# A fused mixer, expert gather and second block: the mixer written for halves of the tokens, the expert loads in groups of four

## The reference, cut to what matters

```python
h = _rmsnorm(x, norm_mix_w)
proj = h @ w_in                       # q, k, v, z, two gates, pool input
qkv = silu(_causal_conv(qkv, conv_w))
o = _chunk_gated_delta_rule(q, k, v, g, beta)
pool_out = _multiscale_pool(p, w_pool, pool_scale)
x = x + concatenate([o, pool_out]) @ w_out
# experts, for each token: 8 heads, 16 experts each, from 128 x 128
q = (xb @ w_query).reshape(t, 8, 2, 128)
scores = einsum("thpc,hpkc->thpk", q, sub_keys)
s1, i1 = top_k(scores[:, :, 0], 16); s2, i2 = top_k(scores[:, :, 1], 16)
top_s, idx = ...                      # the best 16 of the 256 sums s1 + s2
gate = softmax(top_s)
act = gelu(einsum("td,thkd->thk", xb, expert_down[idx]))
x = x + einsum("thk,thkd->td", gate * act, expert_up[idx])
x = _rmsnorm(x, norm_final_w)
```

## Time and profile before

| | before |
|---|---|
| time, median of 3 runs | 2648.42 us (2647.81 to 2650.79) |
| profiled execution, its own time | 2648.01 us |
| its span | 2646.2 us |
| PE, DVE, ACT, POOL busy | 80%, 51%, 31%, 43% of the span |
| DMA | 647.63 MB, mean 245 GB/s |
| granted PE clock, mean | 0.955 |

### The profile page before, as it was taken

How to read it: one execution, slowest core, us unless ns; L and a number is a source line. 1 busy time by engine, 2 the same in 40 slices (tenths; PEclk the granted TensorE clock), 3 DMA queues, 4 the chain that set the end, 5 groups by cost and what they waited for, 6 DMA issues and landing times.

```text
span 2646.2 us, 20923 instructions
## 1 busy us (share of the span) xinstructions
PE 2120.1 (80%) x7148; PEld 1243.0 (47%) x7148; DVE 1349.2 (51%) x2765; ACT 810.2 (31%) x1865; POOL 1143.9 (43%) x826
## 2 busy tenths in 40 slices
PE   7878988957777777777777777777698886999996
PEld 4335945832222222223222232222486655788785
DVE  2446443166676776776776767765401441333301
ACT  2121212223333333333333333332423552222212
POOL 6971681344444444444444444443342002344442
PEclk8987998979999999999999999999798998999998
DMA  5441032159999999999999999997221001122221
GB/s 203 143 151 72 29 120 76 55 220 421 421 421 421 421 421 421 421 421 421 422 421 421 421 421 419 422 416 328 96 96 64 1 0 64 64 96 96 96 96 48
DMA packets 90443, 647.63 MB, mean 245 GB/s; under 512 B 10208, under 2 KB 10208, under 8 KB 19808
## 3 DMA queue, kind: packets, MB, share of 16 engines
q0 software_dynamic: 73728, 536.90, 48.8%
q1 hardware_dynamic: 16608, 109.39, 11.4%
HBM read 644.16 MB, written 2.10 MB: 244 GB/s over the span
## 4 chain that ended last, share of the span: by engine, by line
PE 48%; DMA 37%; DVE 7%; ACT 5%; POOL 2%; issue 1%; ACTq 0%; DVEq 0%; SPq 0%; POOLq 0%; PEldq 0%
PE ps L426 47%; DMA arena<-in_experts,arena_u 36%; DVE arena L1331 2%; ACT arena L873 1%; ACT sel L867 1%; ACT upper L961 1%; PE ps L385 1%; ACT arena L375 1%; DVE arena L1246 0%; DVE arena L1390 0%; DVE x L1391 0%; POOL gtrow L1009 0%; ACT sel L864 0%; DMA arena<-in_w_early 0%; DMA x<-in_x 0%
## 5 line engine op out<-in xcount | busy, mean ns | idle before, releaser
L426 PE MATMUL ps<-arena 128*128 128x512 f32 (+1 forms) x3536 | 1325.2, 524 | 406.7 <-ACT arena L873 347.7
L426 PEld LDWEIGHTS ps<-arena 128*128 128x128 f32 x3536 | 590.7, 194 | 1120.2 <-ACT arena L873 552.8
L1080 POOL DMA_INDIRECT arena<-in_experts,arena_u x512 | 601.6, 1175 | 693.5 <-PE ps L426 582.8
L1331 DVE CUSTOM_DVE_ANT_0 arena<-arena 128x1024 f32<-128x1024 f32 x512 | 627.4, 1225 | 374.2 <-DMA arena<-in_experts,arena_u 370.7
L426 PE MATMUL ps<-r_low 128*128 128x512 f32 x2208 | 511.3, 393 | 9.2 <-DVE r_low L1352 7.6
L1089 POOL TENSOR_TENSOR r_low<-middle,r_low 128x1024 fp32r<-128x1024 f32 x98 | 235.6, 2404 | 544.5 <-ACT r_low L905 544.5
L426 PEld LDWEIGHTS ps<-r_low 128*128 128x128 f32 x2208 | 415.6, 189 | 98.6 <-issue 6.5
L864 ACT ACTIVATE sel<-sel 128x2 f32<-128x2 f32 x256 | 52.1, 203 | 805.2 <-DVE sel L1331 805.2
L905 ACT ACTIVATE r_low<-middle 128x1024 fp32r<-128x1024 f32 x98 | 103.6, 1058 | 280.4 <-PE ps L426 280.3
L873 ACT ACTIVATE arena<-consts,sel 128x128 f32<-128x128 f32 x512 | 177.5, 394 | 23.5
L867 ACT ACTIVATE sel<-sel,arena 128x1 f32<-128x1 f32 x512 | 122.7, 286 | 8.4
(11 more groups left out here) (183 smaller groups left out, 1492.7 us busy)
## 6 DMA issues: line engine op xcount, KB each, us to landing
middle<-in_w_late SPq DMA_DIRECT2D x24, 2048.0 KB, 7.7
gtrow<-in_w_ada SPq DMA_DIRECT2D x32, 512.0 KB, 3.8
arena<-in_w_early SPq DMA_DIRECT2D x7, 2048.0 KB, 11.6
arena<-in_w_ada SPq DMA_DIRECT2D x32, 256.0 KB, 2.8
middle<-in_w_early SPq DMA_DIRECT2D x4, 2048.0 KB, 7.8
arena<-in_experts,arena_u POOLq DMA_INDIRECT x512, 23.9
x<-in_x SPq DMA_DIRECT2D x1, 2048.0 KB, 8.1
arena<-in_rows SPq DMA_DIRECT2D x1, 2048.0 KB, 7.1
```

The lines of the kernel that those rows point to most:

```text
L426: return nc.tensor.matmul(out_, lhsT, rhs, start=start, stop=stop_, skip_group_check=skip)
L1080: nc.gpsimd.indirect_dma_start(ring[n % RING], None, a["experts"], bass.IndirectOffsetOnAxis(ap=idxq[:, i, k:k + 1], axis=0),).then_inc(ga ...
L1331: ins = nc.vector.tensor_tensor_reduce(r[:, 0:D], r[:, 0:D], xn[:, i // PH, :], 1.0, 0.0, ALU.mult, ALU.add, dots[:, g:g + 1])
```

## The change

The mixer and the query are written for half of the tokens (`SH` = 256 columns, two chunks), as a list of small stages (`STAGES`, made by `front_plan`), which every engine walks in the same order. The first half's stages up to query unit 6 stand ahead of the gather. The rest of that query, and then all stages of the second half, are dealt out over the gather: a stage carries the number of the load behind which it comes (`at`), and each engine does the stages due after its work for that load. The last stand at load 241; the second half's tokens are first needed for heads from 16 on. The second half reads all weights again, in units of 512 KB. The query's split is gone, its units are plain fp32 products. silu and sigmoid are made from tanh.

A load now takes four experts for 32 tokens: its 128 rows are 32 tokens x 4 experts, `xn` is spread so that 32 tokens stand four times (`xrep`, for each tile by 32 small products and 8 copies), the indices are moved to that order by a small product (`permute`), and a load's sums go to 32 partitions of the banks. The number of loads and their bytes stay. The ring has 8 buffers instead of 13, freed in fours, and one pair of banks serves all tiles. SP may fetch the first late chunks once all scores of the second half are written.

```diff
-RING = 13
-PAIR = 2
+RING = 8
+GROUP = 4
...
+def paced(plans):
+    at, beside, out = 0, False, []
+    for after, h, stage, arg in plans:
+        beside = beside or (h == 0 and stage == "q" and arg == 7)
+        at += after if beside else 0
+        out.append((at if beside else -1, h, stage, arg))
+    return out
+
+STAGES = paced(front_plan(0) + front_plan(1))
+
+class Pace:
+    def upto(self, n):
+        while self.at is not None and self.at <= n:
+            self.at = next(self.program, None)
...
-                pe.wait_ge(s["diag"], PAIR * (m + 1))
-                for k in range(PAIR * m, PAIR * m + PAIR):
-                    for n in range(2):
-                        ins = mm(ps[:, bank + n, :], diag[:, k % 8, :], ring[k % RING][:, D + n * HALF:D + (n + 1) * HALF],
-                                 False, k % (PH * TOPK) == PH * TOPK - 1, True)
-                ins.then_inc(s["slot_done"], PAIR)
...
+                pe.wait_ge(s["diag"], n + 1)
+                for h in range(2):
+                    for k in range(n - GROUP + 1, n + 1):
+                        j = k % 4
+                        ins = mm(ps[32 * j:32 * j + 32, 6 + h, :], diag[:, m % 4, 32 * j:32 * j + 32],
+                                 ring[k % RING][:, D + h * HALF:D + (h + 1) * HALF], False, m % (4 * PH) == 4 * PH - 1, True)
+                ins.then_inc(s["slot_done"], GROUP)
+
+            for n in range(LOADS):
+                i, t, j = n // TOPK, n // (TOPK * PH), n % 4
+                turn = n % (TOPK * PH) >= TOPK * PH - 4 and t < T - 1
+                if turn and j < 3:
+                    spread_rows(t + 1, j)
+                elif not turn and n % TOPK == TOPK - 1 and i + 2 < HEADS:
+                    permute(i + 2, t + 1)
+                if n % GROUP == GROUP - 1:
+                    sums(n)
+                if turn and j == 3:
+                    spread_rows(t + 1, 3)
+                    permute(i + 2, t + 2)
+                front.upto(n)
...
+            for n in range(RING, LOADS, GROUP):
+                front.upto(n - RING + GROUP - 2)
+                for k in range(n, n + GROUP):
+                    load(k)
...
+                    nc.vector.tensor_tensor_reduce(r[:, 0:D], r[:, 0:D], xrep[k % 4], 1.0, 0.0, ALU.mult, ALU.add,
+                                                   dots[:, n % 8:n % 8 + 1]).then_inc(s["dots"], 1)
+                    if k == 0 and 1 <= i < HEADS - 1:
+                        place(i + 1)
+                    next(ahead, None)
+                    front.upto(n)
...
-            sp.wait_ge(s["acc_out"], T)
+            sp.wait_ge(s["gates_out"], N_GATE)
+            sp.wait_ge(s["scs"], 2 * Q_UNITS)
+            sp.dma_start(prow_fin, a["prow"][1:2, :].broadcast_to([P, D])).then_inc(s["pfin"], 16)
             for m in range(LATE):
```

1766 lines of the change are left out of this document (1109 added, 657 removed).

## The result

The changed kernel takes 2680.79 us (median of 4 runs, 2678.38 to 2684.14) beside 2648.43 for the kernel before: a ratio of 1.0121, 95% interval 1.0107 to 1.0135, so it is 1.2% slower where 5.9% faster was forecast. The profiled execution has a span of 2677.5 us, 187.5 over the 2490 of the forecast.

The account below looks back on a forecast made before the run. It saw three serial parts: 558.3 us with idle DMA, a 1294.9 us DMA-bound gather, 793.0 behind. First issue 280, gather 1416, rest 793 and 1 gave span 2490, time about 2492 us, 5.9% less; range 2440 to 2620.

Parts of the forecast that it names:

- Part 1, the first load: Mixer and query ahead of the gather: first load issued at 280 us instead of 558.3, a gain of 278.
- rival 4: Mixer ahead of the gather: halves don't gain, first issue at 400 or later, 2612 us; chance 0.01.
- the last pair of weights is requested only when the output projection is done ... another 10: Modulation weights in the first half: the last pair is waited for ahead of the query, 10 us.
- Part 2, the extra bytes: Gather's DMA: 44.6 MB carried beside the loads' 537 MB, 106 us at 421 GB/s.
- Part 3, the ring: Gather's ring of 8 buffers in fours: DMA's 9.96 us a group rules while the product block is below 4.7.
- rival 3: Gather's narrow products: four strips run one after another, block of 7.4 us, 2823 us in all; chance 0.14.
- 3.1 until data flows; 9.96 for the four transfers: Ring turn's formula: time from issue until data flows, then the transfers of a group's four loads.
- The clock: TensorE in the gather: mostly the lower clock level expected behind load 241, granted clock below 0.9.
- Part 4, the shared stretch: Second half beside the gather, loads 19 to 241: every engine fits on average, none with much room.
- 20 us for such waits, 0 to 100: Second half beside the gather: engines waiting in their own order, 20 us taken, 0 to 100 possible.
- rival 2: Shared stretch: ring starves, one engine's wait per group on the return path, 108 us more, 2600; chance 0.20.
- 7.3 + 4.7 = 12.0, while DMA needs 13.3: POOL in the shared stretch: up to three gate steps plus four issues fit within DMA's time, in us.

Follow-up runs that it names:

- e1: Changed kernel with all 32 modulation rows, and their weight-pair requests, written ahead of the output projection: 2639.23 us.
- e10: Changed kernel with only the two late weight chunks requested after the last sum, not beside the gather: 2671.25 us.
- e6: Kernel before with 8 ring buffers instead of 13, and GpSimd's wait rounded up to multiples of four sums: 2799.70 us.
- e5: Kernel before with 8 ring buffers instead of 13, sums still over two loads: 2653.24 us.
- e4: Changed kernel with twelve buffers instead of eight from load 272 on, late chunks requested after the last sum: 2630.85 us.
- e7: Changed kernel with four unread 128x512 products of constants behind each group of sums from load 272 on, to raise TensorE's clock: 2673.13 us.
- e2: Changed kernel with the second half's 32 gate rows dealt behind every fourth paced stage instead of every one: 2652.54 us.
- e8: Changed kernel with the edits of e1, e2 and e4 together: 2570.34 us.
- e14: e8 with 28 of 32 gate rows' GpSimd operations cut to one column (output not the reference's): 2558.38 us.
- e12: e8 with the second half's 44 weight units transferred at an eighth of their columns (output not the reference's): 2546.20 us.
- e9: e8 with sums over two loads instead of four: 2577.27 us.
- e15: e8 with the second half's projection units paced at three loads instead of two, and twelve buffers from load 296: 2592.54 us.

## Why the prediction was wrong

**Part 1, the first load.** The direction held, and rival 4 (halves don't gain) is refuted: 231 us earlier. PE's 200 us were 237 busy, at 72% instead of 82%. The step that failed is "the last pair of weights is requested only when the output projection is done ... another 10": not one pair but nine rows were late, and they held PE itself. It cost 35 us of the 47, by e1. I had seen the wait and priced it from one request, without following who stands behind whom in SP's list.

**Part 2, the extra bytes.** Right in size: the GB/s of the gather's stretches times their lengths make 583 MB, 46 more than the loads' 537, against 44.6. "Prefetching the late chunks returns nothing" was right as well, and by e10 it costs about its whole 10 us.

**Part 3, the ring.** The unknown that I had spent most words on came out well: eight narrow products take 3.68 us on the chain at a low clock, inside the room of 4.7, and rival 3 (strips one after another, 7.4) is false. The failed step is the formula beside it, "3.1 until data flows; 9.96 for the four transfers", 13.1 us from a group's first issue to its last landing. In the turn shown it is 15.7 (4.7 and 11.0 by the chain). By the landings the transfers are sized right: the other three follow the first in 7.5. But the first lands 8.2 us after its issue where the formula has 5.6 (3.1 + 2.49, taken from the shortest landing, with an empty queue); the mean over loads 280 to 500 is 7.6. With 15.7 the turn is (2.0 + 3.7 + 0.3 + 15.7) / 2 = 10.8 us a group, not 9.96; 68 groups behind load 241 make 57 us. (The issues of loads 241 and 511 lie 739.2 us apart, 10.95 a group; the two late chunks' 10 us are in that.) e6 shows the same loss in a kernel that has nothing else of the change, e5 that it is not eight buffers alone, e4 that it goes away with more. The forecast asked whether the way round fits into two groups' time, and it did by 0.5 us a group; it didn't ask how much transfer is still queued at the first issue, 4.5 us, which is too little. Why the first load takes 7.6 and not 5.6 to 7.0 (4.5 + 2.49) there is not shown.

**The clock.** Forecast at the lower level behind load 241, and it was (0.60 and 0.59 in the two stretches, with PE busy 36% of the time). On this the trace agrees with the Trainium skill (TensorE: Matmul & The Clock Gate, Part 1, The HAM clock gate), which has the low clock as the default. With a deep ring it cost nothing: e4 moves 413 GB/s at 0.58. In the ring of eight its price is open, since e7 raised the clock in part of the time only.

**Part 4, the shared stretch.** The second failed term is "20 us for such waits, 0 to 100", and this is rival 2's place: of the 145 us that the gather is too long, 57 are the ring's behind load 241, and most of the other 88 went in loads 19 to 241. The average that I made for POOL, "7.3 + 4.7 = 12.0, while DMA needs 13.3", took the gate steps at the earlier trace rows's 1.09 and 1.34 us; beside a busy DVE they took 1.31 and 1.69 on average (28 of each in 400 to 650, the rows shown with e2), and POOL waited 35 us more for their weights. By e2, 28 us of this were the gate rows' place alone. The dot product, taken at 1225 ns, had a mean of 1571 in 500 to 650.

**The sum.** Three edits take 110 us off the changed kernel (e8), which leaves 78 to the forecast: 8 at the first load, 73 in the gather, and 3 less behind it. All of the 73 lie ahead of 1200 us, since from there e8 moves 418 GB/s. Of them e14 gives 14 to the gate rows wherever they stand. e12 shows that the second half's bytes aren't the rest: the transfer's price for them was in the forecast already, and only half of it came back. Finer steps (e9) and a slower pace (e15) brought nothing there. What holds the remaining 60 us stays open. One place to look is the way back from a step's last landing to the next first issue. In e8's loads 24 to 240 the dot product of that last load starts 2.8 us after the landing, against 0.4 behind load 292, with DVE in other work; from its end to the first issue it is 4.5 us against 4.8, although the mean clock is higher there (0.74 to 0.80 against 0.61). So DVE's order is at least as likely a cause as PE's sums standing behind units of the second half; neither was tried.

## What to carry to other kernels

In a ring of buffers, ask how much transfer is still queued when a step's first issue is made: (buffers - step) x one load's transfer, less the way back from landing to issue. Here 4 to 4.5 us lost time in most steps and 8 lost none, and the same eight buffers gave either. A chain that follows the last load shows its issue and its latency, but only the landings of its neighbours tell whether the row of issues was waited for. When work is laid beside a stream, look not only at whether each engine has room on average but at what stands ahead of the stream's issues in the issuing engine's list, including the waits for that work's own weights. And a request is as late as the last wait ahead of it in the queue that makes it. Three small edits took 110 us off here, none of them at the strips that I had doubted.

## What the hardware showed that I had not expected

- Eight products of 32 output columns, four strips side by side, took 3.68 us at the low clock (granted 0.50), although the mean of their sixteen records is 1024 ns: the records overlap fourfold. On this the trace agrees with the Trainium skill (TensorE: Matmul & The Clock Gate, Part 3, Packing small matmuls). Two strips side by side took 1.94 us where four took 1.97, both with the clock granted at 1.00.
- DVE's 128x1024 dot product took 1227 ns where POOL only issued loads (1200 to 1500 us) and up to 1571 on average where POOL had tensor operations; with the gate rows cut to one column it was back at 1246 in 650 to 950 us, from 1418. POOL's 128x512 addition took 1342 ns in the kernel before and up to 1856 on average beside the second half.
- From the first to the fourth of four indirect issues in a row pass 4.0 to 4.7 us (e6, e7 and after), where three of the median 0.938 us would be 2.8: 0.30 us stands behind each, and often one of them takes up to 1.7 us. In a ring with transfer enough in the queue (e4) this row costs nothing.
- A load issued with an empty queue landed after 5.2 to 5.6 us, and with 4.5 us of transfer still to land after 7.6 on average (after, loads 280 to 500), half a us behind the transfer's own pace; with 8.0 or 13.8 us still to land (e5, e4) no such delay shows.
